# Splitting the first query columns ahead of a norm, and taking half of that norm's squares to VectorE

## The reference, cut to what matters

```python
    return _rmsnorm(x, final_norm_g)                 # end of first_block
...
def _rmsnorm(x, g):
    xf = x.astype(jnp.float32)
    y = xf * lax.rsqrt(jnp.mean(xf * xf, axis=-1, keepdims=True) + EPS)
    return (y * g.astype(jnp.float32)).astype(x.dtype)
...
    qkv = (x @ w_qkv).reshape(B, S, 3, H, dh)         # start of the first layer
```

## Time and profile before

| | |
|---|---|
| median of 3 runs | 1335.56 us (1335.51 to 1336.13) |
| profiled execution, its own time | 1339.6 us |
| its span, first to last instruction | 1337.5 us |
| TensorE busy | 1181.4 us, 88% |
| VectorE busy | 691.7 us, 52% |
| ScalarE busy | 491.0 us, 37% |
| mean granted TensorE clock | 0.954 |

### The profile page before, as it was taken

How to read it: one execution, slowest core, us unless ns; L and a number is a source line. 1 busy time by engine, 2 the same in 40 slices (tenths; PEclk the granted TensorE clock), 3 DMA queues, 4 the chain that set the end, 5 groups by cost and what they waited for, 6 DMA issues and landing times.

```text
span 1337.5 us, 22105 instructions
## 1 busy us (share of the span) xinstructions
PE 1181.4 (88%) x9371; PEld 922.3 (69%) x9371; DVE 691.7 (52%) x1045; ACT 491.0 (37%) x711; POOL 3.9 (0%) x8
## 2 busy tenths in 40 slices
PE   6999999999876757667676899999999999999997
PEld 5688888886543324333343699888888899888886
DVE  4689967774211101010120567586666767766666
ACT  5653456554110100000000454554444456544442
POOL 0000000000000000000000000000000000000000
PEclk9999999998998878887897999999999999999999
DMA  9867587689999999999999864434636345463610
GB/s 357 282 218 269 185 307 267 240 324 369 426 424 426 428 429 426 426 429 429 427 429 422 302 252 152 164 142 173 229 149 230 103 159 189 158 242 136 242 72 32
DMA packets 92454, 369.92 MB, mean 277 GB/s; under 512 B 6622, under 2 KB 14604, under 8 KB 79316
## 3 DMA queue, kind: packets, MB, share of 16 engines
q1 hardware_dynamic: 91992, 367.92, 70.4%
q10 hardware_dynamic: 380, 0.81, 0.2%
HBM read 367.66 MB, written 1.05 MB: 276 GB/s over the span
## 4 chain that ended last, share of the span: by engine, by line
PE 70%; DMA 22%; DVE 4%; ACT 2%; issue 1%; SPq 1%; DVEq 0%; ACTq 0%
DMA arena<-in_moe_w 18%; PE ring L2159 8%; PE ring L2619 6%; PE ring L2148 5%; PE acc L2256 5%; PE acc L2257 5%; PE acc L2258 4%; PE ring L2161 4%; PE ring L2150 2%; DMA own<-in_moe_w 2%; PE acc L2132 2%; PE acc L2133 2%; PE acc L2134 2%; PE ring L2647 1%; PE ring L2304 1%
## 5 line engine op out<-in xcount | busy, mean ns | idle before, releaser
L2619 PE MATMUL ring<-arena 128*32 128x256 f32 x1984 | 148.1, 464 | 66.8 <-DMA arena<-in_moe_w 66.8
L2619 PEld LDWEIGHTS ring<-arena 128*32 128x32 f32 x1984 | 75.6, 132 | 134.9 <-issue 73.4
L1383 DVE TENSOR_TENSOR wlo<-arena,whi 128x2048 fp32r<-128x2048 f32 x56 | 128.0, 2290 | 49.9 <-ACT whi L914 49.9
L1833 DVE TENSOR_TENSOR arena<-arena,ring 128x128 f32<-128x128 f32 x32 | 12.2, 380 | 246.8 <-ACT arena L1187 246.8
L1187 ACT ACTIVATE arena<-ring 128x128 f32<-128x128 f32 x32 | 8.9, 277 | 341.1 <-PE ring L2619 337.6
L914 ACT ACTIVATE whi<-arena 128x2048 fp32r<-128x2048 f32 x56 | 106.8, 1910 | 42.1 <-PE acc L2258 25.4
L2159 PE MATMUL ring<-xboth,whi 128*128 128x512 f32 x320 | 113.8, 398 | 0.0
L2161 PE MATMUL ring<-xboth,wlo 128*128 128x256 f32 x320 | 89.8, 281 | 0.0
L2159 PEld LDWEIGHTS ring<-xboth,whi 128*128 128x128 f32 x320 | 60.1, 188 | 14.6
L2148 PE MATMUL ring<-hboth,w1hi 128*128 128x512 f32 x192 | 68.1, 399 | 0.1
L2657 PE MATMUL acc<-above 32*128 32x256 f32 x512 | 46.0, 426 | 24.4 <-DVE above L1840 16.6
(11 more groups left out here) (439 smaller groups left out, 2689.0 us busy)
## 6 DMA issues: line engine op xcount, KB each, us to landing
arena<-in_moe_w SPq DMA_DIRECT2D x76, 2048.0 KB, 21.9
arena<-in_mlp_w_in SPq DMA_DIRECT2D x16, 2048.0 KB, 10.1
arena<-in_mlp_w_out SPq DMA_DIRECT2D x16, 2048.0 KB, 8.1
own<-in_moe_w SPq DMA_DIRECT2D x14, 2048.0 KB, 25.7
arena<-in_w_in SPq DMA_DIRECT2D x9, 2048.0 KB, 8.3
arena<-in_w_mod SPq DMA_DIRECT2D x6, 2048.0 KB, 12.9
arena<-in_moe_w SPq DMA_DIRECT2D x10, 1024.0 KB, 15.7
own<-in_w_mod SPq DMA_DIRECT2D x4, 2048.0 KB, 11.0
```

What stands on the lines that cost most here:

```text
L1383: dve.tensor_tensor(lo, raw, hi.bitcast(F32), ALU.subtract).then_inc(G["split_ready"], 1)
L2619: ins = pe.matmul(o, xs[:, kt, j, :], w[kt][g], start=(kt == 0), stop=(kt == KT - 1))
```

## The change

ScalarE, in the passage: it waits for the last product but one of the experts, splits the query columns, and only then waits for the puts; then it squares tile 0 alone. The root of tile 1 is taken of a mean square that VectorE makes. VectorE first makes the first half of the query columns' low part, then, when the puts are done, the moments of tile 1 (two `bn_stats` over 512 columns each, one `bn_aggr`, and mean x mean + variance), then the products of the norm, and after them the second half of the low part. The half tiles are multiplied, turned and copied in the order 0, 2, 1, 3: the first column half of both tiles, then the second. So the first product's blocks 0 to 3 wait for two high parts and no longer for three. The later passages keep the order 0, 1, 2, 3.

```diff
+def turned_order(n):
+
+    return (0, 2, 1, 3) if n == 0 else (0, 1, 2, 3)
...
-    order += [("xT", (0, i), "V") for i in range(4)]
+    order += [("xT", (0, i), "V") for i in turned_order(0)]
...
-                act.wait_ge(G["ssq_ready"], TT * n + tt + 1)
+                act.wait_ge(G["ssq_ready"], TT * n + tt + (n < 2))
...
-            for tt in range(TT):
-                act.wait_ge(G["put_done"], 8 * NE)
-                token_std(1, tt, acc[:, tt, :], squared[1], 0)
+            act.wait_ge(bank_full, turn_full(TURNS - 1, "down", EXPERTS_PER_TURN - 2))
             split_hi(MIXER_HALVES)
-            for i in range(4):
+            act.wait_ge(G["put_done"], 8 * NE)
+            token_std(1, 0, acc[:, 0, :], squared[1], 0)
+            act.wait_ge(last_squares, 1)
+            act.activation(lstd[:, 1:2], lss[:, 1:2], ACT.Sqrt, bias=oeps[:, 0:1]).then_inc(G["lstd_ready"], 1)
+            for i in turned_order(0):
                 x_high(0, i)
...
+            raw, hi, lo = half_of(MIXER_HALVES)
+
+            def low_of_half(j):
+                return dve.tensor_tensor(in_half(lo, j), of_half(raw, j), in_half(hi.bitcast(F32), j), ALU.subtract)
+
+            dve.wait_ge(G["whi_ready"], MIXER_HALVES + 1)
+            low_of_half(0)
+            dve.wait_ge(G["put_done"], 8 * NE)
+            for q, f in enumerate(half):
+                dve.bn_stats(parts_of_tile[:, q, :], acc[:, 1, f]).then_inc(parts_made, 1)
+            dve.wait_ge(parts_made, 2)
+            dve.bn_aggr(moments[:, :], parts_of_tile[:, :, :].rearrange("p q s -> p (q s)")).then_inc(moments_made, 1)
+            dve.wait_ge(moments_made, 1)
+            dve.scalar_tensor_tensor(lss[:, 1:2], moments[:, 0:1], moments[:, 0:1], moments[:, 1:2], ALU.mult, ALU.add).then_inc(last_squares, 1)
             dve.wait_ge(fin_in, 16)
-            for tt in range(TT):
-                rstd(1, tt)
-                for f in half:
-                    dve.scalar_tensor_tensor(hres[:, tt, f], acc[:, tt, f], lrstd[:, tt:tt + 1], fin_g[:, f], ALU.mult, ALU.mult).then_inc(G["ht_ready"], 1)
-            split_lo(MIXER_HALVES)
-            for i in range(4):
+            for i in turned_order(0):
+                tt, q = divmod(i, 2)
+                if q == 0:
+                    rstd(1, tt)
+                f = half[q]
+                dve.scalar_tensor_tensor(hres[:, tt, f], acc[:, tt, f], lrstd[:, tt:tt + 1], fin_g[:, f], ALU.mult, ALU.mult).then_inc(G["ht_ready"], 1)
+            low_of_half(1).then_inc(G["split_ready"], 1)
+            for i in turned_order(0):
                 x_low(0, i)
...
-                for i in range(4):
+                for turn_, i in enumerate(turned_order(n - 1)):
                     tt, q = divmod(i, 2)
                     b = bank(name, (n - 1, i) if name == "xT" else i)
-                    if i in KEPT[n]:
+                    if turn_ in KEPT[n]:
                         kept_busy(b, 2 if n == 1 else 3)
-                    pe.wait_ge(G["ht_ready"], 4 * n + i + 1)
+                    pe.wait_ge(G["ht_ready"], 4 * n + turn_ + 1)
```

More of the change, by code:

```diff
@@ L431, in build @@
         ssum = sb("ssum", [P, TT, MOBA_H])
+        parts_of_tile = sb("parts_of_tile", [P, TT, 6])
+        moments = sb("moments", [P, 2])
         share = sb("share", [P, TT, MOBA_H])
@@ L454, in build @@
         masks_in = sem("masks_in")
+        parts_made = sem("partial_moments_of_last_tile")
+        moments_made = sem("moments_of_last_tile")
+        last_squares = sem("mean_square_of_last_tile")
         first_up_read = sem("first_expert_slab_read")
@@ L1872, in x_low @@
                 b = bank_of("xT", (n, i)).rearrange("p (k t) -> p k t", k=4)
-                dve.wait_ge(G["xhi_ready"], 4 * n + i + 1)
+                dve.wait_ge(G["xhi_ready"], 4 * n + turned_order(n).index(i) + 1)
                 v = xhi[:, 4 * q:4 * q + 4, tt * P:(tt + 1) * P].bitcast(F32)
                 dve.tensor_tensor(xlo[:, 4 * q:4 * q + 4, tt * P:(tt + 1) * P], b, v, ALU.subtract).then_inc(freed["V"], 1)
-            dve.wait_ge(fin_in, 16)
-            for tt in range(TT):
-                rstd(1, tt)
-                for f in half:
-                    dve.scalar_tensor_tensor(hres[:, tt, f], acc[:, tt, f], lrstd[:, tt:tt + 1], fin_g[:, f], ALU.mult, ALU.mult).then_inc(G["ht_ready"], 1)
-            split_lo(MIXER_HALVES)
-            for i in range(4):
+            raw, hi, lo = half_of(MIXER_HALVES)
[10 more added lines that the diff above has]
+            dve.scalar_tensor_tensor(lss[:, 1:2], moments[:, 0:1], moments[:, 0:1], moments[:, 1:2], ALU.mult, ALU.add).then_inc(last_squares, 1)
+            dve.wait_ge(fin_in, 16)
+            for i in turned_order(0):
[6 more added lines that the diff above has]
+            for i in turned_order(0):
                 x_low(0, i)
@@ L2175, in first_half @@
                         elif kt % 4 == 0 and w is wh and x is xhi:
-                            pe.wait_ge(G["xhi_ready"], 4 * n + 2 + kt // 4 + 1)
+                            pe.wait_ge(G["xhi_ready"], 4 * n + turned_order(n).index(2 + kt // 4) + 1)
                         for j in range(2):
```

## The result

The change makes the kernel slower. The medians of 8 runs each are 1335.7 us before and 1339.93 us after; the ratio is 1.0028 (95% interval 1.0019 to 1.0036), so 3.7 us (2.5 to 4.8). The profiled execution's span is 1339.5 us against 1337.5, less than that, because the experts before the passage happened to end 1.7 us earlier in it. Read from the start of the occupying matmuls (743.52 after, 745.20 before), which stand right behind the last puts, the passage is longer by the whole amount.

The account below looks back on a forecast made before the run. The prediction took the passage before the first product to be set by ScalarE, VectorE close behind. A product start 2.4 us later plus 2.0 for the fallen clock, 4.4 on 1335.56, gave 1340.0 us, range 1336.6 to 1341.8.

Parts of the forecast that it names:

- Late columns: ScalarE's early split waits for query columns landing at 745.41, starts at 745.46 uncovered by experts; root 0 2 us later.
- VectorE as the chain: VectorE's low half, then bn_stats and small steps, come last before the norm; reciprocal 0 starts 3.41 us late.
- Start of the product with a full clock: TensorE's first product starts at 754.1 against 751.68, +2.4 us, with the clock held.
- The clock: TensorE's idle stretch of 4.2 us before the first turn drops the clock to half, costing +2.0 us.
- The sum: Whole passage: 2.4 + 2.0 = 4.4 us on 1335.56, giving 1340.0 us.
- Columns in time: Rival: query columns land by 743.4, so the product starts 0.8 us early, 1334.8; chance 0.08.
- Moments dear: Rival: VectorE's bn_stats and small steps at their upper bounds, +1.4 us, 1341.4, up to 1342.3; chance 0.08.

Follow-up runs that it names:

- the stretch filled: Changed kernel with six occupying matmuls instead of two ahead of the first turn; timed +2.3 us (+1.1 to +3.3) against the kernel before.
- low halves behind: Changed kernel with both low halves behind the norm on VectorE, ScalarE's split still ahead; timed +2.1 us (+0.9 to +3.3) against the kernel before.
- split alone: Kernel before with only the query columns' split moved ahead, high and first low half; timed +1.5 us (+0.3 to +2.7) against the kernel before.

## Why the prediction was right

**Late columns.** The prediction had the split start at 745.46 with the puts ending at 745.42. In the trace after it starts 0.22 us behind the occupying matmuls, as predicted (0.26). In the other runs with the early split and the transfer in place it starts 0.19 to 0.27 us behind them, so the landing of this one trace was no chance. The run without the transfer shows that this wait, and not the new instructions, makes the loss.

**VectorE as the chain.** The low half took 1.14 us to its successor (1.15), the two bn_stats 1.29 (1.31), from there to the first reciprocal 748.61 - 746.91 = 1.70 us (1.75). The nearest rows were good prices for an operation that the trace did not show. The first reciprocal was 3.33 us late (3.41).

**Start of the product with a full clock.** Forecast +2.4, measured +2.25 with the stretch filled. The gain that this contains was forecast as 0.82, all of it from the order; with the split behind the norm, or the columns in time, it is 0.90. Its source was only partly right. Where the split stands behind the norm, 0.55 us are there without the order (S - O of 5.93 against 6.48) and the order adds 0.35. No run has the whole change with the order 0, 1, 2, 3, so the order's share in the changed kernel itself is not shown.

**The clock.** That it would fall was read from 16 of 16 stretches in the earlier trace rows, and it fell. The size was the one term clearly off: 2.0 forecast, 16.05 - 14.55 = 1.50 measured. Of this the turns were to lose 1.1 and lost 0.75: four turns took 0.85 us each at half clock, close to the 0.66 in which VectorE fed them, and not the 1.0 of the forecast, by which the four would even have lost 751.37 + 4.0 - 754.1 = 1.3. The product lost 0.75 of 0.9. Reckoning all throttled time at the part of the clock that is missing would have been further off here. The clock was at its lower level for some 6.8 us (from near 747.8 to near 754.6, by the windows), half of which is 3.4. But during 1.8 us of that TensorE did nothing, and over the turns it was slowed by VectorE as well. So the Trainium skill's rule (TensorE: Matmul & The Clock Gate, section Terms) gives more than twice what this stretch cost. The agreement that the prediction saw on the run of the earlier trace rows is one over its busy part alone. In the trace before, the clock falls at 703.3, in the idle stretch ahead of that run (0.81 granted over 703.0 to 703.5, 0.50 behind it), and is back near 713.5. These 10.2 us would cost 5.1 by the rule, where 2.76 were lost. In both places the rule fits the part at half clock in which nothing else paced TensorE: 2.8 us for 2.76 there, 0.8 for 0.75 in the first 1.6 us of the product here.

**The sum.** 3.75 us by the passage against 4.4, so 0.65 too much, 0.50 of it the clock and 0.15 the start of the product. That the median of 1339.93 lies next to the forecast 1340.0 is luck: the median before was 0.14 us higher over 8 runs than over the 3 of the forecast, and the two medians differ by 4.2 us, more than the passage moved.

**The rivals.** Columns in time was worth -0.8 in the forecast and -0.89 in the run that stands for it. The landing that the forecast named for it, 743.4, was wrong: split and low half take 3.2 us from the landing by its own figures (745.41 to 748.62), so they are done by 745.42 only if the columns land by 742.2. Its break-even of 743.0 fits that figure and not 743.4; no run has a landing in between. With the clock held, +2.4 was forecast, and +2.25 measured once it was made to hold. Moments dear did not come about. What the forecast did not look at was what comes next: where both low halves of the query columns stand behind the norm and the clock stays up, VectorE's low part of the key columns holds the second product by 0.27 to 0.64 us more than before (N - O less S - O, in four runs). It had no part in this result: in the changed kernel that distance is 6.57 us, and with the stretch filled it is 5.82, as before.

## What to carry to other kernels

Work that is moved ahead of a wait gains only if its own input is there by then: before moving a split up, set the landing of its transfer beside the end of what is to cover it. Here the two waits end within 0.1 us of each other, and in a queue in program order that puts the whole moved piece, 2 us, in front of the critical one. And when a change delays the engine that feeds TensorE, look at the idle stretch it opens: if filling matmuls are there for the old one, they must grow with it, which here would have given back 1.5 of 3.75 us.

## What the runs showed of the hardware

A `bn_stats` over 128x512 of the accumulator banks costs 0.65 us of VectorE, about as much as the 0.69 us of a tensor_tensor over the same elements, and the aggregate of two of them 0.21 us.

Idle stretches of like length were not answered alike. With 4.10 us of idling the clock fell within the stretch, and with 2.72 us (low halves behind) also within it, before the first turn at 746.37:

```profile
745.00:746.00 1.00, 0.00 (x0) 0.85 1.10 367
```

With 2.65 us (split alone) it fell only once the turns had begun:

```profile
746.00:747.00 1.00, 0.00 (x0) 1.00 1.10 364
747.00:748.00 1.00, 0.19 (x2) 1.00 1.08 353
748.00:749.00 1.00, 0.91 (x8) 1.00 1.03 301
749.00:750.00 1.00, 0.77 (x6) 0.89 1.09 365
750.00:751.00 1.00, 1.00 (x6) 0.50 1.12 370
```

So a stretch that looks survived, by a clock of 1.00 at its end, may still be paid for in the product behind it: 1.0 us here. Before, the same turns behind 0.78 us of idling kept the clock. Each of these is one execution, and why the two nearly equal stretches differ is not shown.
